# Hybrid conv/pool decoder block: the conv output's transposes moved from TensorE to the DMA crossbar

## The chip, the cores and the metric

The kernel runs on all 8 cores of one Trainium2 chip. Each core computes 2048 of the 16384 token rows (four sequences of 4096, half a sequence per core) and needs nothing from the other cores; a core that has the second half of a sequence also gets the 32 rows before it. The metric is the device time in microseconds (us) of the slowest core.

## What is computed

The reference, cut to the branch that matters here (`C_CONV` = 1024 channels):

```python
def conformer_conv_branch(u_glu, dw_kernel, dw_bias, ln_g, ln_b, w_out):
    a, gate = jnp.split(u_glu, 2, axis=-1)
    u = a * jax.nn.sigmoid(gate)
    u = depthwise_causal_conv(u, dw_kernel, dw_bias)   # width 31
    u = layer_norm(u, ln_g, ln_b)                      # per token, over channels
    u = jax.nn.swish(u)
    return u @ w_out
...
merged = g_conv * y_conv + g_pool * y_pool
h = h + rms_norm(merged @ w_o, mix_post_g)
```

`y_pool` comes from a pooling branch of the same projection, `g_conv` and `g_pool` are sigmoid gates, and a squared-ReLU MLP of width 4096 follows.

## The kernel before, in words

All of it is one program per core. A small recorder (class `KB`) keeps one list of instructions for each engine in the order in which the Python code emits them, works out from the memory cells which semaphore waits each needs, and emits the lists. So an engine (and each DMA queue: SP's for `LOAD` and `DTR`, POOL's for `WLOAD`) does its work strictly in program order, and an instruction that waits holds up all behind it on the same engine. TensorE's matmuls are recorded at line 220 (`MM`) and its transposes, which are matmuls against an identity, at line 223 (`TR`); ScalarE's activations at line 238; the crossbar transposes, issued from SP, at line 263 (`DTR`).

The stages in order: RMS norm and transposes of x; pooling projection; GLU projection (`glu_pair`), whose result goes through `DTR` (`conv_in`, lines 567 to 572: for each of 8 channel slabs one transpose of a 16-partition halo and one of a 128 x 2048 tile); the depthwise conv as matmuls (`cv_mm`); then the stage of this change, lines 724 to 747; then the conv branch's projection, the output projection and the MLP.

The conv leaves its output in `cv`, indexed [partition m, slab cc, r, channel c], where the token is 16 m + r. There tokens lie on the partitions, which suits the layer norm: `ln_stat`, `ln_fin` and `ln_norm` run on VectorE from a list of background steps (`bgd`), of which `pump(n)` does the next n; there are 16 `ln_norm` steps, one for each r, over all slabs. The projection after it (`wco`) needs channels on the partitions: that is `s_t`, which lies in the same memory as `cv`, slab for slab.

The stage itself is the first pass of `gated` (line 684), 4 token blocks by 8 output slabs, 32 calls, here numbered 0 to 31 (number 8 blk + cc). Each call has two times 8 matmuls of 128 x 512 on `weff` and `wgp`, into a pair of the 8 PSUM banks; then a tanh on ScalarE (line 691) and one VectorE operation that multiplies (line 694), after which the pair is free again. Call n+4 uses the pair of call n.

In blocks 2 and 3, after every odd cc (calls 17, 19, ..., 31), `cv_t3` (line 711) handles one slab: 16 TensorE transposes of 128 x 128 into two PSUM banks, then two ScalarE activations that compute silu with the layer norm's gain and bias and write the slab of `s_t` in place. The last slab follows call 31, and right behind it the second pass begins (line 840): `gated` on `wco` and `s_t`, whose first 8 matmuls read slabs 0 to 7 in turn.

Behind the first pass SP's queue has `LOAD(gb1)`, `LOAD(gb2)` (lines 750, 751) and three loads of x (line 755). `gb1` lies at the start of the scratch region `TP`.

Of the kernel before, what the change touches and what calls it, by code (L numbers as in the profile page):

```python
# [8 lines left out]
BF16 = mybir.dt.bfloat16  # L9
AF = mybir.ActivationFunctionType  # L10
# [16 lines left out]
TP = RM + 8 * NT  # L27
# [143 lines left out]
def build_program():  # L171
# [20 lines left out]
    with ExitStack() as es:  # L192
# [3 lines left out]
        identb = T("identb", [128, 128], BF16)  # L196
# [7 lines left out]
        ps = es.enter_context(nc.psum_tensor("ps", [128, 8, 512], F32))  # L204
        kb = KB()

        def av(off, *dims, dt=BF16):
            n = int(np.prod(dims))
            v = arena[:, off:off + (n if dt is BF16 else 2 * n)]
            if dt is not BF16:  # L210
                v = v.bitcast(dt)
            if len(dims) > 1:
                names = ["d%d" % i for i in range(len(dims))]
                v = v.rearrange("p (" + " ".join(names) + ") -> p " + " ".join(names),
                                **{a: d for a, d in zip(names[:-1], dims)})
            return v
# [5 lines left out]
        def TR(o, i, idn):  # L222
            kb.op("pe", lambda e: e.transpose(o, i, idn), [i, idn], [o])  # L223

        def ACT(o, i, func, bias=None, scale=None, accum=None):
            kw = {}
            rd, wr = [i], [o]
            if bias is not None:
                kw["bias"] = bias
                rd.append(bias)  # L230
            if scale is not None:
                kw["scale"] = scale
                if not isinstance(scale, float):
                    rd.append(scale)
            if accum is not None:
                kw["accum_out"] = accum
                wr.append(accum)
            kb.op("act", lambda e: e.activation(out=o, in_=i, func=func, **kw), rd, wr)  # L238
# [22 lines left out]
        def DTR(o, i):  # L261

            return kb.op("sp", lambda e: e.dma_start_transpose(out=o, in_=i), [i], [o], dma=True)

        def WLOAD(o, src, after=()):
            return kb.op("pool", lambda e: e.dma_start(out=o, in_=src), [], [o], dma=True, after=after)  # L266
# [3 lines left out]
        def banks(n):  # L270
            b = -(-st["bank"] // n) * n % 8
            st["bank"] = (b + n) % 8
            return b
# [9 lines left out]
        cv = av(RS, 8, 16, 128)  # L283
        s_t = av(RS, 8, NT)
# [3 lines left out]
        def slot(i, *dims):  # L288
            return av(RW + i * SLOT, *dims)
# [15 lines left out]
        kc = [av(RW + 4608 + b * 768, 48, 16) for b in range(2)]  # L305
        hg = [av(TP + b * 2048, 2048)[0:16, :] for b in range(2)]
        Wc = slot(6, 16, 3, 128)
        bias_bc = av(RW + 7 * SLOT + 2048, 1024, dt=F32)
        pwT = av(RW + SLOT + 2048, 4, 2, 256)
        pwf = av(RM + 4096, 4, 2, 256, dt=F32)  # L310
# [75 lines left out]
        def vcol(base, cc):  # L386
            return vec[:, base + cc:base + cc + 1]
# [51 lines left out]
        def pump(n):  # L439
            for _ in range(n):  # L440
                if bgd:
                    bgd.popleft()()
# [163 lines left out]
        def ln_stat(half, r):  # L606
            i = cv[:, 4 * half:4 * half + 4, r, :]
            o = bnst[:, r, half, :]
            kb.op("dve", lambda e: e.bn_stats(o, i), [i], [o])  # L609
# [5 lines left out]
        def conv_steps(pair):  # L615

            def spread(cc, cs):
                for c in cs:
                    cv_w(cc, c)

            def fin(cc):
                if cc + 2 < 8:
                    conv_load(cc + 2)
                cv_mm(cc)

            out = []
            for cc in (2 * pair, 2 * pair + 1):
                out += [lambda cc=cc: spread(cc, (0, 1, 2)), lambda cc=cc: spread(cc, (3, 4, 5)),
                        lambda cc=cc: spread(cc, (6, 7)), lambda cc=cc: fin(cc)]
            return out  # L630
# [53 lines left out]
        def gated(cc, blk, wy, src, wgate, first):  # L684
            b = banks(2)
            for k in range(8):
                MM(ps[:, b, :], wy[:, k, cc * 128:(cc + 1) * 128], src[:, k, blk * 512:(blk + 1) * 512], k == 0, k == 7)
            for k in range(8):
                MM(ps[:, b + 1, :], wgate[:, k, cc * 128:(cc + 1) * 128], uT[:, k, H + blk * 512:H + (blk + 1) * 512], k == 0, k == 7)
            sg = sigslot()  # L690
            ACT(sg, ps[:, b + 1, :], AF.Tanh, scale=0.5)
            m = m1(blk, cc)
            if first:
                STT(m, sg, 1.0, ps[:, b, :], ALU.add, ALU.mult)
            else:
                STT(sg, sg, 1.0, ps[:, b, :], ALU.add, ALU.mult)
                TTE("dve", m, sg, m, ALU.add)
# [9 lines left out]
        def ln_norm(r):  # L707
            v = cv[:, :, r, :]
            TS(v, v, bnag[:, r, 0:1], ALU.subtract, lnr[:, r:r + 1], ALU.mult)

        def cv_t3(cc):
            sv = s_t[:, cc, :].rearrange("p (m r) -> p m r", r=16)
            pbs = []
            for half in range(2):
                b = banks(1)
                pb = ps[:, b, :].bitcast(BF16)
                pbs.append(pb)
                for r8 in range(8):
                    TR(pb[:, r8 * 128:(r8 + 1) * 128], cv[:, cc, half * 8 + r8, :], identb[:])
            for half in range(2):  # L720
                ACT(sv[:, :, half * 8:half * 8 + 8], pbs[half].rearrange("p (r m) -> p m r", r=8), AF.Silu,
                    bias=vcol(8, cc), scale=vcol(0, cc))

        for blk in range(4):
            steps = deque(conv_steps(3) if blk == 0 else [])
            for cc in range(8):
                gated(cc, blk, weff, z, wgp, True)
                if blk == 0:
                    pump(2)
                    if cc == 0:  # L730
                        steps.popleft()()
                        steps.popleft()()
                    if steps:
                        steps.popleft()()
                    if cc == 6:
                        for r in range(16):
                            bgd.append(lambda r=r: ln_stat(1, r))
                        bgd.append(ln_fin)
                        for r in range(16):
                            bgd.append(lambda r=r: ln_norm(r))  # L740
                elif blk == 1:
                    pump(5)
                elif cc % 2 == 1:
                    cv_t3((blk - 2) * 4 + cc // 2)
            if blk == 0:
                WLOAD(wgc, w_in_v[:, :, 3072:4096])
                WLOAD(wo, wo_v)
# [247 lines left out]
```

How the kernel before makes its waits and increments, by code:

```python
            def body(h, items=items):  # L156
                for waits, fn, ev, dma in items:
                    for sk, v in waits.items():
                        h.wait_ge(sems[sk], rank[sk][v] if sk in rank else v)
                    if fn is None:
                        continue
                    inst = fn(h)
                    if dma:
                        inst.then_inc(sems[ev[0]], 16)
                    elif ev[1] in rank[ev[0]]:
                        inst.then_inc(sems[ev[0]], 1)
```

## Time and profile before

| | us |
|---|---|
| runs of the kernel, median of three | 975.74 |
| the profiled execution's own time | 976.0 |
| its span, first to last instruction, slowest core | 974.4 |
| spans of the 8 cores | 971.7 to 974.4 |
| TensorE busy within the span | 949.2 |

The profile shows one execution. The span is some 1.6 us shorter than that execution's own time, and this execution lies 0.3 us above the median of the three runs. A busy TensorE means that matmuls were in its pipeline; one matmul's listed duration overlaps the next one's, so the cost of a group on the path is read from the starts of the groups, or from the chain of waits, and not from the mean duration. TensorE's granted clock was 1.00 in the stage of the change, the higher of its two levels (2.4 GHz).

### The profile page before, as it was taken

What the parts mean: (1) busy time and instruction counts of PE and PEld (TensorE: products, weight loads), DVE (VectorE), ACT (ScalarE), POOL (GpSimd) and SP (SyncE); (2) the same over time, 40 slices, a digit from 0 to 9 for tenths busy, and PEclk for the clock granted to TensorE, in tenths of its full rate; (3) what the DMA queues carried; (4) which work ended last, traced back from release to release, by engine and by line L of the source; (5) the groups of instructions that cost most, each with busy time, mean ns of one, the idle gap of its engine ahead of it and who ended that gap; (6) DMA issues with size and microseconds to landing.
All of it is one profiled execution on the core that took longest, in us unless ns stands there. A gap on an engine that the chain in (4) does not pass through costs nothing.

```text
span 974.4 us, 14114 instructions; the slowest of 8 cores (971.7 to 974.4 us)
## 1 busy us (share of the span) xinstructions
PE 949.2 (97%) x4971; PEld 484.2 (50%) x4971; DVE 451.3 (46%) x767; ACT 277.6 (28%) x531; POOL 62.6 (6%) x112
## 2 busy tenths in 40 slices
PE   7789999999999999999999999999999999999996
PEld 4655666665545544444444444444444444444444
DVE  4478886575482114566666630344223431244222
ACT  4553111132114431333335530233202330133211
POOL 1010001000010000121213200000000000000000
PEclk9999999999999999999999999999999999999999
DMA  9995165976780021759989995220022001210021
GB/s 183 253 146 74 17 89 105 143 109 115 118 140 1 1 87 15 143 117 191 168 190 178 196 197 90 87 87 1 1 87 87 1 1 44 87 43 1 1 86 66
DMA packets 93111, 91.21 MB, mean 94 GB/s; under 512 B 43601, under 2 KB 74577, under 8 KB 92914
## 3 DMA queue, kind: packets, MB, share of 16 engines
q0 software_dynamic: 32416, 35.13, 26.2%
q1 hardware_dynamic: 60626, 55.18, 21.1%
q8 instruction: 41, 0.67, 0.3%
q14 instruction: 28, 0.23, 0.1%
HBM read 98.88 MB, written 16.84 MB: 119 GB/s over the span
## 4 chain that ended last, share of the span: by engine, by line
PE 91%; DMA 3%; DVE 3%; ACT 1%; issue 1%; DVEq 0%; ACTq 0%; SPq 0%
PE ps L220 90%; DMA arena<-w_in 2%; DMA arena<-xh 1%; ACT arena L238 1%; PE ps L223 1%; DVE arena L246 1%; DVE arena L250 1%; DVE arena L477 0%; DMA arena<-arena 0%; DVE arena L241 0%; ACT sm L238 0%; DVE arena L256 0%; DVEq L159 0%; DVE sm L400 0%; ACTq L159 0%
## 5 line engine op out<-in xcount | busy, mean ns | idle before, releaser
L220 PE MATMUL ps<-arena 128*128 128x512 bf16 (+4 forms) x4731 | 937.9, 360 | 13.9 <-DVE arena L246 2.8
L220 PEld LDWEIGHTS ps<-arena 128*128 128x128 bf16 (+1 forms) x4731 | 470.1, 103 | 473.4 <-issue 25.7
L238 ACT ACTIVATE arena<-ps 128x512 bf16<-128x512 f32 (+5 forms) x346 | 203.0, 593 | 622.1 <-PE ps L220 467.0
L246 DVE TENSOR_SCALAR ps<-ps 128x512 f32<-128x512 f32 x128 | 89.1, 699 | 110.9 <-PE ps L220 110.2
L241 DVE TENSOR_TENSOR ps<-ps,arena 128x512 f32<-128x512 f32 (+1 forms) x65 | 43.6, 688 | 176.1 <-ACT arena L238 175.6
L250 DVE SCALAR_TENSOR_TENSOR arena<-arena,ps 128x512 bf16<-128x512 f32 (+1 forms) x64 | 43.9, 686 | 133.0 <-ACT arena L238 111.0
L241 DVE TENSOR_TENSOR arena<-ps,arena 128x512 bf16<-128x512 f32 (+2 forms) x52 | 42.3, 830 | 35.6 <-ACT arena L238 29.6
L238 ACT ACTIVATE arena<-arena 128x1024 bf16<-128x1024 f32 (+1 forms) x33 | 34.8, 1054 | 46.3 <-DVE arena L250 35.8
L250 DVE SCALAR_TENSOR_TENSOR arena<-ps,sm,arena 128x512 f32<-128x512 f32 (+1 forms) x65 | 45.1, 737 | 5.0 <-DVE sm L400 3.0
L250 DVE SCALAR_TENSOR_TENSOR arena<-arena,sm 128x1024 bf16<-128x1024 f32 (+1 forms) x33 | 42.3, 1282 | 4.3 <-POOL sm L396 2.4
L241 DVE TENSOR_TENSOR arena<-arena 128x512 bf16<-128x512 f32 (+2 forms) x56 | 38.4, 690 | 4.3
L246 DVE TENSOR_SCALAR arena<-arena,vec 128x768 bf16<-128x768 bf16 (+1 forms) x72 | 27.7, 413 | 2.7
L266 POOL DMA_DIRECT2D arena<-w_in x14 | 12.6, 909 | 156.7 <-DMA arena<-arena 137.3
L223 PE MATMUL ps<-identb,arena 128*128 128x128 bf16 (+1 forms) x240 | 16.9, 220 | 3.7 <-DVE arena L250 2.1
L266 POOL DMA_DIRECT2D arena<-w_ff x16 | 13.5, 852 | 106.7 <-PE ps L220 99.4
L238 ACT ACTIVATE arena<-ps,vec 128x1024 bf16<-128x1024 bf16 x16 | 19.3, 1204 | 2.5 <-PE ps L223 1.7
L609 DVE BATCH_NORM_STATS2 bnst<-arena 128x6 f32<-128x512 bf16 x32 | 19.9, 679 | 0.0
L223 PEld LDWEIGHTS ps<-identb,arena 128*128 128x128 bf16 (+1 forms) x240 | 14.9, 99 | 9.0 <-issue 5.8
L400 DVE RECIPROCAL sm<-sm 128x1 f32<-128x1 f32 (+1 forms) x33 | 5.3, 162 | 29.2 <-ACT sm L238 17.4
L396 POOL TENSOR_TENSOR sm<-sm,mhalf 128x1 f32<-128x1 f32 x32 | 18.2, 567 | 5.0 <-POOL sm L395 0.4
L250 DVE SCALAR_TENSOR_TENSOR arena<-arena 128x512 bf16<-128x512 f32 x24 | 16.5, 687 | 1.2
L477 DVE TENSOR_TENSOR_SCAN arena<-arena,scr 128x512 f32<-128x512 f32 x12 | 15.3, 1278 | 3.6 <-ACT arena L238 3.6
(34 smaller groups left out, 91.3 us busy)
## 6 DMA issues: line engine op xcount, KB each, us to landing
arena<-xh SPq DMA_DIRECT2D x32, 512.0 KB, 8.6
arena<-w_ff POOLq DMA_DIRECT2D x16, 1024.0 KB, 27.8
out<-arena SPq DMA_DIRECT2D x31, 512.0 KB, 3.1
arena<-out SPq DMA_DIRECT2D x16, 512.0 KB, 4.1
arena<-w_in POOLq DMA_DIRECT2D x12, 512.0 KB, 13.1
arena<-w_in POOLq DMA_DIRECT2D x2, 2048.0 KB, 17.2
arena<-gb SPq DMA_DIRECT2D x4, 512.0 KB, 6.4
arena<-w_pool_out POOLq DMA_DIRECT2D x2, 1024.0 KB, 23.1
```

The lines of the kernel that those rows point to most:

```text
L220: kb.op("pe", lambda e: e.matmul(o, lhsT=l, rhs=r, start=start, stop=stop), [l, r], [o])
L223: kb.op("pe", lambda e: e.transpose(o, i, idn), [i, idn], [o])
L238: kb.op("act", lambda e: e.activation(out=o, in_=i, func=func, **kw), rd, wr)
L241: kb.op(eng, lambda e: e.tensor_tensor(out=o, in0=a, in1=b, op=op), [a, b], [o])
L246: kb.op("dve", lambda e: e.tensor_scalar(out=o, in0=a, scalar1=s1, scalar2=s2, op0=op0, **kw), rd, [o])
L250: kb.op("dve", lambda e: e.scalar_tensor_tensor(out=o, in0=a, scalar=s, in1=b, op0=op0, op1=op1), rd, [o])
L266: return kb.op("pool", lambda e: e.dma_start(out=o, in_=src), [], [o], dma=True, after=after)
L396: kb.op("pool", lambda e: e.tensor_tensor(out=o, in0=o, in1=mhalf[:, 0:n], op=ALU.pow), [o, mhalf[:, 0:n]], [o])
L400: kb.op("dve", lambda e: e.reciprocal(o, o), [o], [o])
L477: kb.op("dve", lambda e: e.tensor_tensor_scan(so, pc[:, lo:lo + n], pc[:, lo - w:lo - w + n], init, ALU.add, ALU.subtract), rd, [so])
L609: kb.op("dve", lambda e: e.bn_stats(o, i), [i], [o])
```

## The change

`cv_t3` issues one crossbar transpose (`DTR`) of a whole 128 x 2048 slab, from SP, into one of two new buffers `s_r`, and a new function `silu` computes the activation from that buffer in one ScalarE instruction of 2048 elements per partition. The buffers lie at the start of `TP` (the first one where `gb1` is loaded later). The first two slabs are sent off after call 15, the last of block 1, behind a `pump(32)` that does any normalization step still left. From call 18 to call 25, each call is followed by the silu of one slab (0 to 7) and the transpose of the slab two further on, which goes into the buffer that this silu has read.

```diff
+        s_r = [av(TP + b * 2048, 16, 128) for b in range(2)]
...
         def cv_t3(cc):
-            sv = s_t[:, cc, :].rearrange("p (m r) -> p m r", r=16)
-            pbs = []
-            for half in range(2):
-                b = banks(1)
-                pb = ps[:, b, :].bitcast(BF16)
-                pbs.append(pb)
-                for r8 in range(8):
-                    TR(pb[:, r8 * 128:(r8 + 1) * 128], cv[:, cc, half * 8 + r8, :], identb[:])
-            for half in range(2):
-                ACT(sv[:, :, half * 8:half * 8 + 8], pbs[half].rearrange("p (r m) -> p m r", r=8), AF.Silu,
-                    bias=vcol(8, cc), scale=vcol(0, cc))
+
+            DTR(s_r[cc % 2], cv[:, cc, :, :].rearrange("p r c -> p (r c)"))
+
+        def silu(cc):
+            ACT(s_t[:, cc, :].rearrange("p (m r) -> p m r", r=16), s_r[cc % 2].rearrange("p r m -> p m r"), AF.Silu, bias=vcol(8, cc), scale=vcol(0, cc))
...
                 elif blk == 1:
                     pump(5)
-                elif cc % 2 == 1:
-                    cv_t3((blk - 2) * 4 + cc // 2)
+                    if cc == 7:
+                        pump(32)
+                        cv_t3(0)
+                        cv_t3(1)
+                elif 8 * blk + cc in range(18, 26):
+                    n = 8 * blk + cc - 18
+                    silu(n)
+                    if n + 2 < 8:
+                        cv_t3(n + 2)
```

## Rows read from the trace of the kernel before

**Rows 1.** The page's part 1: busy time, share of the span, instructions.

```profile
PE 949.2 (97%) x4971; PEld 484.2 (50%) x4971; DVE 451.3 (46%) x767; ACT 277.6 (28%) x531; POOL 62.6 (6%) x112
```

**Rows 2.** TensorE's waits, 358 to 970 us: total us, times, longest.

```profile
PE ps L220 <- ACT arena L238: 1.2, 1, 1.2
```

**Rows 3.** Chain of waits, 290 to 370 us: start, us on the chain, what.

```profile
299.86 0.89 PE ps L223 x16
300.75 6.91 PE ps L220 x32
...
354.46 0.91 PE ps L223 x16
...
355.45 1.21 ACT arena L238
...
356.75 1.21 ACT arena L238
```

**Rows 4.** Timeline of TensorE, 352 to 372 us: start, us, what, idle before.

```profile
355.19 1.67 PE L220 MATMUL ps<-arena 128*128 128x512 bf16 x7
358.10 14.19 PE L220 MATMUL ps<-arena 128*128 128x512 bf16 x65 [1.24 <-ACT arena L238]
```

**Rows 5.** Timeline of VectorE, 255 to 355 us.

```profile
293.43 0.55 DVE L246 TENSOR_SCALAR arena<-arena,bnag,lnr 128x1024 bf16<-128x1024 bf16 x1
300.84 0.69 DVE L250 SCALAR_TENSOR_TENSOR arena<-arena,ps 128x512 bf16<-128x512 f32 x1 [2.77 <-PE ps L223]
```

**Rows 6.** Line 263, crossbar transposes, fastest and slowest of eight 128 x 2048 ones.

```profile
L263 SPq DMA_TRANSPOSE arena<-arena x1: 2056/2056/2056, 158.5 to 158.5; - x1
DMA to landing us min/median/max: 4.3/4.3/4.3
...
L263 SPq DMA_TRANSPOSE arena<-arena x1: 1992/1992/1992, 124.3 to 124.3; - x1
DMA to landing us min/median/max: 5.8/5.8/5.8
```

**Rows 7.** Stretches: busy us of each engine, clock, DMA share, GB/s.

```profile
194.00:202.00 8.00, 8.00 (x39) 5.05 (x38) 5.20 (x11) 3.13 (x4) 0.00 (x0) 1.00 0.42 78
292.00:316.00 24.00, 24.00 (x146) 12.22 (x145) 6.06 (x11) 9.96 (x12) 0.00 (x0) 1.00 0.00 1
316.00:340.00 24.00, 24.00 (x153) 12.45 (x151) 4.35 (x7) 11.17 (x14) 0.00 (x0) 1.00 0.00 1
```

**Rows 8.** DMA issues, 259 to 292 us, KB, us to landing; timeline of POOL.

```profile
260.40 0.88 POOL L266 DMA_DIRECT2D arena<-w_o  x1 [0.25 <-issue]
...
arena<-w_o POOLq DMA_DIRECT2D x1, 2048.0 KB, 29.2
```

**Rows 9.** Groups by line and shape, 292 to 358 us: busy us, mean ns.

```profile
L238 ACT ACTIVATE arena<-ps,vec 128x1024 bf16<-128x1024 bf16 x16 | 19.3, 1204 | 2.5 <-PE ps L223 1.7
```

**Rows 10.** The page's part 5: activations that read SBUF.

```profile
L238 ACT ACTIVATE arena<-arena 128x1024 bf16<-128x1024 f32 (+1 forms) x33 | 34.8, 1054 | 46.3 <-DVE arena L250 35.8
```

**Rows 11.** Timeline of ScalarE, 299 to 306 us.

```profile
300.07 0.60 ACT L238 ACTIVATE arena<-ps 128x512 f32<-128x512 f32 x1 [2.86 <-PE ps L220]
300.83 1.28 ACT L238 ACT_TABLE_LOAD   x1 [0.17 <-PE ps L223]
```

**Rows 12.** Timeline of SP's queue, 120 to 130 and 180 to 355 us.

```profile
119.03 7.22 SPq L263 DMA_TRANSPOSE arena<-arena  x3
...
236.89 116.27 SPq L259 DMA_DIRECT2D arena<-gb  x2
353.20 2.27 SPq L259 DMA_DIRECT2D arena<-xh  x3
```

**Rows 13.** Line 263, the slowest 128 x 1024 transpose, and queues, 480 to 490 us.

```profile
L263 SPq DMA_TRANSPOSE arena<-arena x1: 3954/3954/3954, 483.8 to 483.8; - x1
DMA to landing us min/median/max: 12.6/12.6/12.6
...
q0 software_dynamic: 1157, 1.17, 92.0%
```

## The prediction

> **What bounds the kernel now.** I read the busy times first: TensorE is busy 97% of the span, VectorE 46%, ScalarE 28% [rows 1]. So the end is set by how much work TensorE has and by the few places where it waits, and the reader should look at nothing else until TensorE has been accounted for. Second, TensorE's waits: behind 358 us it waits once, for 1.2 us [rows 2]. Whatever moves 358 us earlier moves the end earlier by as much, unless a new wait appears. Third, the chain of waits through the stage of the change. It alternates strictly between two groups: 32 matmuls (two `gated` calls) for 6.91 us, and the 16 transposes of a slab for 0.89 us [rows 3]. There are eight such transpose groups, the last of 0.91 us. So the transposes are not hidden, they stand on the chain between matmuls. Last, TensorE's own timeline at the end of the stage: after the last transposes it does 7 matmuls of the second pass, slabs 0 to 6, and stands still for 1.24 us until ScalarE has finished the two silus of slab 7, 1.21 us each on the chain [rows 3, 4].
>
> **What the change takes away.** The 128 transposes: 7 x 0.89 + 0.91 = 7.14 us of chain [rows 3]. Their listed durations would give another figure, because matmuls overlap; the chain has the price. Then the stall before the second pass, 1.24 us [rows 4]: it exists because slab 7 is transposed behind the last call, and the new order has its silu six calls earlier. Together 8.38 us. Nothing else is late at that point: `wco` was loaded before this stage, `wgc` and `wo` too (29.2 us after an issue at 260.4 us, so by 290 us [rows 8]).
>
> The two PSUM banks that each slab took are no longer allocated; eight slabs took 16, two full turns of eight, so every later call gets the banks it had.
>
> **What it adds, and why I cost it at nothing.** Four parts.
>
> *The start.* `pump(32)` has nothing to do: the list's last normalization runs at 293.43 us for 0.55 us, in the slot of call 14 [rows 5]. So SP may issue slab 0 at 294.0. Call 17 ends at 299.70 us and its tanh starts at 300.07 [rows 11]; a call takes 6.91 / 2 = 3.45 us [rows 3]. Call 18's tanh, with no transposes ahead, is due at 303.52.
>
> *The transposes.* The same kernel already sends eight 128 x 2048 tiles through the crossbar (`conv_in`). They take 4.7, 5.8, 4.7, 4.3, 4.7, 5.5, 4.7 and 4.4 us from issue to landing, mean 4.85, fastest and slowest in [rows 6]; the issue itself holds SP some 2 us. I take 4.9. These ran beside other traffic: the engines were 42% busy while a few of them passed, and in the new place they are 0% busy [rows 7], so contention should be lower. Bounds for the landing: the fastest of the eight below, 4.3 us, and above the slowest crossbar transpose of the trace, 12.6 us, for a tile of half the size while weight loads kept the engines 92% busy [rows 13].
>
> A rule that speaks against this step: the Trainium skill, page "VectorE: DVE Perf Modes", section "The three transpose paths", lists 390 ns for a 128 x 128 bf16 transpose on TensorE and 1309 ns through the DMA crossbar, and its rules for authors send such a transpose to TensorE wherever a PSUM destination will do. By that price a slab of 16 blocks would take 16 x 1.309 = 20.9 us if they pass one after another, an estimate from that page. The trace disagrees with both figures: 0.89 / 16 = 0.056 us for a block on TensorE [rows 3] and at most 5.8 us for a slab [rows 6].
>
> *ScalarE.* Sixteen silus of 1.204 us go [rows 9], eight of 2048 elements come. Below: a 1024-element activation from SBUF takes 1.054 us and a 512-element tanh 0.60 [rows 10, 11], so 0.45 us per 512 elements and 1.054 + 2 x 0.45 = 1.95 us. Above: the trace shows no activation that reads SBUF in 256-byte steps; were each element to cost double, 2 x 1.95 = 3.9. Two of the present silus, which read PSUM in the same pattern, make 2.41, and I take 2.4 as the nearest row. With a tanh of 0.60 that is 3.0 of the 3.45 us of a call: ScalarE fits, narrowly. The table load of 1.28 us before the first silu stays [rows 11].
>
> *The loop.* The new wait is a ring: a silu waits for its slab, and the transpose two further on waits for that silu. One turn is 4.9 + 2.4 = 7.3 us, while two calls take 6.9. So the silus drift by 0.4 us per turn. Behind a waiting silu stands the next call's tanh, behind that the VectorE operation, behind that the PSUM pair, which TensorE needs four calls later. Step by step: tanh 18 ends at 304.12, table load to 305.40, silu 0 to 307.8; slab 2 lands at 312.7 (silu due 311.0), slab 4 at 320.0, slab 6 at 327.3, silu 6 ends at 329.7. The tanh of call 25 behind it was due at 327.67: 2.0 us late, the worst of all. In general, with landing time L, this tanh is 0.83 + 3 x (L - 4.5) us late. What can it afford? A pair is normally free when the VectorE operation ends, 300.84 + 0.69 = 301.53 for call 17, 1.83 us after its last matmul [rows 5], and is needed three calls later, 10.35 us. Slack 8.5 us, against 2.0 used. So TensorE does not see the ring at all until L passes 7.1 us. Slab 7's silu ends at about 332.7, and the second pass now starts near 348.0 (299.70 + 14 x 3.45): 15 us to spare.
>
> *SP's queue.* Behind the six waiting transposes stand `gb1`, `gb2` and three loads of x. `gb1` now waits for silu 6, near 330 us; `gb2` waited for the matmuls of the stage's end anyway and held the x loads until 353.2 us [rows 12]. They follow TensorE as before. POOL's queue has no load in this stage. If that cover were gone, the first output tile would wait for them, but it comes a whole block later.
>
> **The sum.** Against the profiled execution: 976.0 - 7.14 - 1.24 = 967.6 us. That execution lies 0.3 us above the median of the three runs, so by the median it would be 967.4; I keep 967.6. The gain is 0.9%, below the 2% that a measurement of this kernel can tell from no change.
>
> **Rivals.**
>
> *A. The ring is too slow (slower side).* Landing takes 12.6 us, as for the transpose beside the weight loads [rows 13]. Then tanh 25 is 0.83 + 3 x 8.1 = 25.1 us late, 16.6 beyond the slack, and the time is 967.6 + 16.6 = 984.2. It decides from L = 7.1 us on, and the gain is all gone at 16.9 us of lateness, L = 9.9. Against it: the DMA engines idle in this stage [rows 7], and no 128 x 2048 tile took over 5.8 us. Chance 0.05.
>
> *B. Slabs pass one at a time.* If the crossbar did not overlap or start them sooner, at 12.6 us each the eighth lands at 294.0 + 8 x 12.6 = 394.8, its silu ends at 397.2, call 26's pair is free 1.5 us later, at 398.7, and call 30, due at 341.1, waits 57.6 us: 1025. Against it: the rows named under A, and from 119.0 us on SP issued three transposes in 7.2 us [rows 12], the last of them the slowest of the eight [rows 6]; one after another at 12.6 us does not fit that. Chance 0.02. By the estimate of 20.9 us from the Trainium skill's page above this would be 8 x 8.3 = 66 us worse still; the trace's 5.8 us speaks against it.
>
> *C. Part is given back.* Silus of 3.9 us, or landings near 8 us: a ring turn of 4.9 + 3.9 = 8.8 us drifts 1.9 per turn, and ScalarE at 3.9 + 0.6 = 4.5 us per call falls 1.05 us per call behind, 8 us over the stage. With the table load that is about 9 to 10 us late, 1 to 2 beyond the slack; L = 8 gives 11.3 late, 2.8 beyond. Time 968.5 to 970.5. For it: ScalarE fits only narrowly. Chance 0.08.
>
> *D. The end does not move.* Something later, now 8.4 us sooner, waits for a transfer that starts at its old time: 976. Against it: behind 358 us TensorE has no such wait [rows 2], and the loads follow it. Chance 0.03.
>
> **How the numbers follow.** The forecast, 967.6, has 0.82. Its own spread is small: the chain terms are read to 0.02 us each, runs differ by about 0.5 us. The range takes in C and some unseen cost: 966.3 to 971.5; outside lie A, B and D (0.10) and the tails. Faster by over 2% (below 956.2) would need more than the stage holds: 0.01. Slower by over 2% (above 995.3) is B and a bad part of A: 0.03. Within 2%: 0.96.
>
> **What would show it.** Right: no transposes between the matmul groups from 299 us on; two calls every 6.91 us through calls 16 to 31; no wait of TensorE before the second pass, which starts near 348; eight transposes on line 263 between 294 and 326 us landing in 4.3 to 5.8 us; eight silus near 2.4 us; some tanhs up to 2 us late; TensorE's total busy time some 7 us lower. Wrong: landings over 7 us, silus over 3 us, or TensorE waiting for VectorE or ScalarE between 310 and 345 us.

## The result, and the profile after

The changed kernel takes 967.84 us (median of four runs), the kernel before 975.67 (median of four). The ratio is 0.9918 with a 95% interval of 0.9898 to 0.9937: some 7.8 to 8.0 us less, clear of zero, and below the 2% at which a verdict of faster is given. One of the four executions of before took 1109.9 us in a slow state that some executions of any kernel fall into, with a lower granted clock on some cores; the ratio leaves it out. The profiled execution took 967.8 us; its slowest core, core 0, has a span of 966.3 us. The forecast was 967.6.

A total that fits does not show that its terms fit. One of them was badly off here, and the profile shows which. First the page's part 1 of the changed kernel:

```profile
PE 937.5 (97%) x4758; PEld 477.7 (49%) x4843; DVE 451.8 (47%) x767; ACT 287.9 (30%) x523; POOL 62.5 (6%) x112
```

Against [rows 1], TensorE lost 11.7 us of busy time, but this must not be read as a gain. 4731 weight loads of line 220 are listed and only 4646 of its matmuls: 85 matmul records are missing in this trace. ScalarE is the surprise: eight activations fewer, and 10.3 us more busy time. The groups by line and shape from 292 to 350 us, core 0, say why (busy us, mean ns of one; then the idle time before them and what ended it):

```profile
L220 PE MATMUL ps<-arena 128*128 128x512 bf16 x258 | 57.0, 379 | 1.4 <-DVE arena L250 1.2
L238 ACT ACTIVATE arena<-arena,vec 128x2048 bf16<-128x2048 bf16 x8 | 31.3, 3918 | 1.7 <-DMA arena<-arena 1.7
```

A silu of 2048 elements takes 3.92 us, not the 2.4 that I took, where two of the old ones took 2.41 [rows 9]. And TensorE waits for 1.2 us, for VectorE's line 250, which the forecast said it would not. Its timeline on core 0:

```profile
284.64 51.53 PE L220 MATMUL ps<-arena 128*128 128x512 bf16 x233
336.67 3.61 PE L220 MATMUL ps<-arena 128*128 128x512 bf16 x16 [0.50 <-DVE arena L250]
340.96 34.26 PE L220 MATMUL ps<-arena 128*128 128x512 bf16 x155 [0.67 <-DVE arena L250]
```

The transposes between the matmuls and the stall of 1.24 us before the second pass [rows 3, 4] are gone, and two shorter waits have come at another place. The same view on core 1 has no wait at all:

```profile
284.74 90.60 PE L220 MATMUL ps<-arena 128*128 128x512 bf16 x419
```

So the cores differ. A measure that all have: the time from the tanh of call 17 (the last before the first silu in either kernel) to the tanh of call 32, the first of the second pass, read from each core's ScalarE timeline. I call it the stage. Without any wait it is 15 calls of 3.453 us, 51.80 us. It varies far less than whole runs do: the time at which the stage begins differs by up to 2.8 us between the cores of one of these two executions. Each figure below is read from one profiled execution.

| | stage, 8 cores (us) | median | TensorE waits in it (us) |
|---|---|---|---|
| before | 60.28 to 60.29 | 60.29 | 1.2 on each core |
| after | 53.30, 51.80, 52.42, 51.89, 51.80, 51.83, 52.41, 52.51 | 52.15 | 1.2, 0, 0.5, 0, 0, 0, 0.4, 0.6 |

The stage became 8.14 us shorter at the median, 6.99 to 8.49 by core. Line 263 (the crossbar transposes) in the stage, core 0 and then core 1; the line that begins with ACT says who waited for them, us and times:

```profile
L263 SPq DMA_TRANSPOSE arena<-arena x8: 1693/1962/3721, 292.4 to 331.0; - x8
...
  ACT arena L238: 1.7, 1
...
DMA to landing us min/median/max: 4.2/4.4/6.0
```

```profile
L263 SPq DMA_TRANSPOSE arena<-arena x8: 1746/1990/2852, 292.0 to 329.1; - x8
...
DMA to landing us min/median/max: 4.3/4.4/4.8
```

The landings are close to what the eight of before promised [rows 6]; over all cores those took 4.2 to 6.2 us. On core 0 one of them, slab 2, took 6.0 us; ScalarE waited 1.7 us for it, on core 1 not at all. And ScalarE's timeline on core 1, where TensorE never waits:

```profile
298.06 0.60 ACT L238 ACTIVATE arena<-ps 128x512 f32<-128x512 f32 x1 [2.86 <-PE ps L220]
301.51 0.60 ACT L238 ACTIVATE arena<-ps 128x512 f32<-128x512 f32 x1 [2.86 <-PE ps L220]
302.13 1.28 ACT L238 ACT_TABLE_LOAD   x1
303.43 3.90 ACT L238 ACTIVATE arena<-arena,vec 128x2048 bf16<-128x2048 bf16 x1
...
333.66 3.90 ACT L238 ACTIVATE arena<-arena,vec 128x2048 bf16<-128x2048 bf16 x1
337.47 1.05 ACT L238 ACTIVATE arena<-ps 128x512 f32<-128x512 f32 x2
```

The tanh of call 26 was due at 298.06 + 9 x 3.453 = 329.14 and ran at 337.47, 8.3 us late. Calls 18 to 25 cost ScalarE about 4.3 us each, 0.85 more than TensorE's 3.45; with the table load of 1.28 us before the first silu, eight such calls make 8 x 0.85 + 1.28 = 8.1 us. The slack that the prediction had worked out was 8.5 us. This core came through with 0.2 us to spare; on core 0 the same tanh was 9.9 us late, and TensorE waited.

My reading was then: the two savings are as forecast; silus read in 256-byte steps are slow and nearly fill the slack; whether a core waits is left to the landing of slab 2. The experiments test each part.

### The profile page after: what moved, and what is told of

Read it like the earlier page. It is cut to its first block, busy times and chain, and to the rows that moved or that the text cites. A ratio compares the mean times of both kernels' runs of the same rounds, so it can differ in the third digit from the quotient of the medians.

```text
span 966.3 us, 13780 instructions; the slowest of 8 cores (962.9 to 966.3 us)
## 1 busy us (share of the span) xinstructions
PE 937.5 (97%) x4758; PEld 477.7 (49%) x4843; DVE 451.8 (47%) x767; ACT 287.9 (30%) x523; POOL 62.5 (6%) x112
## 4 chain that ended last, share of the span: by engine, by line
PE 90%; DMA 3%; DVE 2%; ACT 2%; issue 2%; DVEq 0%; ACTq 0%; SPq 0%
PE ps L220 90%; ACT arena L238 2%; DMA arena<-w_in 2%; DMA arena<-xh 1%; DVE arena L241 1%; DVE arena L246 1%; DVE arena L250 0%; PE ps L223 0%; DVE arena L478 0%; ACT sm L238 0%; ACTq L159 0%; DVEq L159 0%; DVE ps L241 0%; DVE arena L256 0%; DVEq L192 0%
## 5 line engine op out<-in xcount | busy, mean ns | idle before, releaser
L238 ACT ACTIVATE arena<-arena,vec 128x2048 bf16<-128x2048 bf16 x8 | 31.3, 3918 | 1.7 <-DMA arena<-arena 1.7
L396 POOL TENSOR_SCALAR sm<-sm 128x1 f32<-128x1 f32 x32 | 7.1, 221 | 133.0 <-DVE sm L241 67.6
L238 ACT ACTIVATE sm<-sm,epst 128x1 f32<-128x1 f32 (+1 forms) x33 | 9.7, 295 | 16.1 <-DVE sm L241 14.5
```

Source lines behind the costliest of these rows:

```text
L396: kb.op("pool", lambda e: e.tensor_scalar(out=o, in0=i, scalar1=EPS[epsc], scalar2=None, op0=ALU.add), [i], [o])
```

## The experiments

There are eight. What tells them apart is the stage, by core, which repeats to 0.01 us where nothing waits.

### The changed kernel again

> No edit: the changed kernel once more, on the same chip as the experiments. Theory (lateness of 8.2 to 8.3 us from the silus, slack 8.5, and a landing of over 4.8 us for slab 2 takes the rest): stage 51.80 us on the cores where that slab lands within 4.8 us and up to 1.5 more where it does not, and which cores these are differs from the first profile or not by the landing alone; whole kernel 966 to 968.5. Rival: the waits belong to fixed cores whatever the landing.

Measured: 967.50 us; stage 51.80 to 52.88, median 51.92. TensorE's waits are not on the same cores: on 3, 5 and 7 now, where the first profile had 0, 2, 6 and 7. The third transpose of each core (slab 2, the one that follows silu 0), from both profiles:

| landing of slab 2 (us) | stage (us) |
|---|---|
| 4.2 to 4.6 (8 cores) | 51.80 to 51.89 |
| 4.7 | 51.98 |
| 5.1, 5.1, 5.2, 5.2 | 52.42, 52.41, 52.51, 52.51 |
| 5.3 | 52.59 |
| 5.6 | 52.88 |
| 6.0 | 53.30 |

Above 4.5 us, and not only above the 4.8 expected, each microsecond of landing is a microsecond of the stage. So it is the landing and not the core that decides (rival out). The landing itself was predicted within bounds; why it scatters between 4.2 and 6.0 us stays open. In these two profiles SP's issue is long too where the landing is (3.7 us on core 0, 1.8 on core 1), but in the contiguous version below that slab landed in 6.0 to 6.1 us on three cores after issues of 1.7 to 1.9 us.

### Four buffers instead of two

```diff
-s_r = [av(TP + b * 2048, 16, 128) for b in range(2)]
+s_r = [av(o, 16, 128) for o in (TP, TP + 2048, RM + 12288, RM + 14336)]
...
-DTR(s_r[cc % 2], ...)
+DTR(s_r[cc % 4], ...)
...
+cv_t3(2)
+cv_t3(3)
...
-if n + 2 < 8:
-    cv_t3(n + 2)
+if n + 4 < 8:
+    cv_t3(n + 4)
```

> Edit: four buffers instead of two, so the transposes run four slabs ahead and the ring is open. Theory R+ring (ScalarE's silus use up 8.3 of the 8.5 us of slack and a slab that lands late adds the rest): no silu waits for a landing, silus stay at 3.92 us, worst tanh about 8.3 us late, no TensorE waits or at most 0.2 us, stage 51.8 us on all cores; whole kernel 966.5 to 967.5. Rival A of the prediction (the ring itself sets the pace): silus still wait for landings, or the lateness falls far below 8 us. Rival S (ScalarE's rate alone is over the slack): waits of TensorE stay near 1.2 us.

Measured: 967.78 us; stage 51.80 on all eight cores, no wait of TensorE on any. Who waited for whom, 298 to 345 us, core 0:

```profile
ACT arena L238 <- PE ps L220: 8.6, 3, 2.9
ACT arena L238 <- DVE arena L250: 0.5, 1, 0.5
```

No line names the DMA any more, though some landings still took 6.0 us. The silus stayed at 3.9 us, and the latest tanh was 8.1 us late on every core. So the ring was not the pace (rival A of the prediction is out); ScalarE's rate is, and it stops just short of the slack (so rival S is out too). The whole kernel lies a little above the 966.5 to 967.5 expected and within 0.1% of the change. That is no contradiction: what the median core had to win was 0.35 us, less than the scatter of the cores' starts.

### Contiguous silu, in two versions

First, the read made contiguous and the write stepped:

```diff
-ACT(s_t[:, cc, :].rearrange("p (m r) -> p m r", r=16), s_r[cc % 2].rearrange("p r m -> p m r"), AF.Silu, ...)
+ACT(s_t[:, cc, :].rearrange("p (m r) -> p r m", r=16), s_r[cc % 2], AF.Silu, ...)
```

> Edit: the silu walks its input in the order in which it lies (contiguous read of the buffer) and writes the slab in 32-byte steps instead. Theory R (the 256-byte-step read is what makes a silu take 3.92 us): the silu falls to 2.0 to 2.4 us, the worst tanh is about 2 us late instead of 8.3 to 9.9, no core waits, tanh of call 17 to tanh of call 32 is 51.8 us on all eight cores (52.15 median, up to 53.30 with the change as made); whole kernel 966 to 967.5. Rival L (2048 elements out of SBUF cost that much in any order, or a strided write costs as much): the silu stays near 3.9 us and four of eight cores keep waits of 0.4 to 1.2 us; 967.8.

Measured: 1009.65 us, ratio 1.0347 (1.0330 to 1.0364); stage 91.7 to 94.7. A clear miss: neither theory had it. Groups from 290 to 400 us, then a piece of TensorE's timeline, both on core 3, the slowest:

```profile
L238 ACT ACTIVATE arena<-arena,vec 128x2048 bf16<-128x2048 bf16 x8 | 71.9, 8993 | 0.0
```

```profile
325.88 6.53 PE L220 MATMUL ps<-arena 128*128 128x512 bf16 x16 [4.67 <-DVE arena L250]
335.19 5.30 PE L220 MATMUL ps<-arena 128*128 128x512 bf16 x16 [2.77 <-DVE arena L250]
```

A silu that writes in 32-byte steps takes 9.0 us. ScalarE then needs 9.3 us per call with a silu, the slack is gone after two of them, and TensorE waits in each later call, 26.8 us in all; 16 matmuls take 5.0 to 6.5 us in place of 3.45 between the waits, at a granted clock of 0.66 to 0.83 averaged over stretches of 10 us (1.00 is its higher level, 0.50 its lower). The slower matmuls do not set the pace: the stretches begin 9.3 us apart (325.88, 335.19) whatever their matmuls take, and that is ScalarE's time per call. This is the price of a lateness that does not fit, paid in full. Since the theory predicted 2.0 to 2.4 us, it had to be asked whether steps are the cause at all. So, both sides contiguous:

```diff
-ACT(s_t[:, cc, :].rearrange("p (m r) -> p m r", r=16), s_r[cc % 2].rearrange("p r m -> p m r"), AF.Silu, ...)
+ACT(s_t[:, cc, :].rearrange("p (r m) -> p r m", r=16), s_r[cc % 2], AF.Silu, ...)
```

> Edit: the silu reads its buffer in the order in which it lies and writes the slab in the same order; this leaves out putting the tokens back in order (the slab stays r-major). Theory R (with the read in 256-byte steps a silu took 3.92 us and with the write in 32-byte steps 9.0 us: steps on either side are what costs): 2048 contiguous elements take 1.95 to 2.1 us, ScalarE needs 2.6 of the 3.45 us of a call, the worst tanh is under 2 us late, no TensorE wait, stage 51.8 us on all cores. Rival L (2048 elements SBUF to SBUF take 3.9 us by their number): silu 3.9 us, tanhs 8 us late.

Measured: 967.10 us, stage 51.80 on all cores. Groups from 296 to 345 us:

```profile
L238 ACT ACTIVATE arena<-arena,vec 128x2048 bf16<-128x2048 bf16 x8 | 16.7, 2091 | 3.4 <-DMA arena<-arena 3.4
```

2.09 us: the 2048 elements from SBUF to SBUF are not dear by number, the steps are. (This version leaves out putting the tokens back in order, so it measures what the steps cost and can't replace the change.) The latest tanh of any core is 2.2 us late, a little over the 2 expected, and silus now do wait for their slabs, 3.4 us in all on this core and up to 6.5 on others. That is the kind of wait the prediction had described for silus of 2.4 us, and it is harmless. But it does not build up: a turn of the ring, 4.4 + 2.1 = 6.5 us, is shorter than two calls, and the waits of silus 2, 4 and 6 on core 4 shrink, 1.35, 1.12 and 0.91 us.

### The silus spread out

```diff
-elif 8 * blk + cc in range(18, 26):
-    n = 8 * blk + cc - 18
+elif 8 * blk + cc in (17, 19, 20, 22, 24, 25, 27, 29):
+    n = (17, 19, 20, 22, 24, 25, 27, 29).index(8 * blk + cc)
```

> Edit: the change with its two buffers, but the silus after calls 17, 19, 20, 22, 24, 25, 27 and 29 instead of 18 to 25. Theory (ScalarE's 4.29 us per call with a silu against TensorE's 3.45 makes the lateness, 0.84 us per call in a row): with 13 calls to carry 8 silus the lateness stays under 4 us, no silu sets a wait of TensorE, stage 51.8 us on all eight cores; whole kernel as with four buffers, 967 to 968. Rival A (landings of the ring set the pace): waits on some cores as before.

Measured: 967.41 us; stage 51.80 on all eight cores. The latest tanh is 2.3 us late on every core, within the 4 us expected. Two buffers and the slow silu are enough if ScalarE has calls without a silu in between. From ScalarE's timeline on core 0, silu 6 and what follows:

```profile
334.33 3.91 ACT L238 ACTIVATE arena<-arena,vec 128x2048 bf16<-128x2048 bf16 x1
338.14 0.59 ACT L238 ACTIVATE arena<-ps 128x512 f32<-128x512 f32 x1
340.74 0.60 ACT L238 ACTIVATE arena<-ps 128x512 f32<-128x512 f32 x1 [2.02 <-PE ps L220]
```

ScalarE waits for TensorE again before the next tanh: it has caught up.

### The order alone, and the crossbar alone

The change has two parts, the way of the transposes and the place of the silus. The kernel before with TensorE's transposes at the new places:

```diff
-elif cc % 2 == 1:
-    cv_t3((blk - 2) * 4 + cc // 2)
+elif 8 * blk + cc in range(18, 26):
+    cv_t3(8 * blk + cc - 18)
```

> Edit: the kernel before with its TensorE transposes and its silus out of PSUM, but one slab after each of calls 18 to 25, as in the change. Theory: only the stall before the second pass goes: stage 60.29 - 1.24 = 59.05 us, whole kernel 974.0 to 975.0; ScalarE has 2.5 + 0.6 us of work in the 4.35 us that a call with a slab takes, so it keeps up. Rival (the order has a price of its own: the transposes' PSUM banks leave the calls only three pairs): new waits of TensorE, stage 59.5 us or more.

Measured: 974.30 us, ratio 0.9983 (0.9973 to 0.9993); stage 58.94 to 58.95 on all cores, no wait of TensorE, so the rival is out. Its timeline on core 3, the slowest:

```profile
303.09 1.06 PE L223 MATMUL ps<-identb,arena 128*128 128x128 bf16 x16
303.98 3.62 PE L220 MATMUL ps<-arena 128*128 128x512 bf16 x16
307.43 1.06 PE L223 MATMUL ps<-identb,arena 128*128 128x128 bf16 x16
...
334.41 37.93 PE L220 MATMUL ps<-arena 128*128 128x512 bf16 x175
```

One call and one transpose group take 307.43 - 303.09 = 4.34 us, 3.45 + 0.89, eight times; then matmuls without a gap into the second pass. The order by itself is worth 60.29 - 58.95 = 1.34 us, and the transposes 58.95 - 51.80 = 7.15.

The crossbar with the silus at the old places:

```diff
-elif 8 * blk + cc in range(18, 26):
-    n = 8 * blk + cc - 18
+elif 8 * blk + cc in (17, 19, 21, 23, 25, 27, 29, 31):
+    n = (17, 19, 21, 23, 25, 27, 29, 31).index(8 * blk + cc)
```

> Edit: the crossbar transposes as in the change, but the silus at the old places, after calls 17, 19, ..., 31. Theory: the transposes' 7.14 us still go, the stall before the second pass comes back and grows, because one silu of 3.92 us takes the place of two that ended 2.73 us after the last transposes: tanh end plus 3.92 puts slab 7 about 5.0 us behind call 31, the 7 matmuls cover 1.5, stall 3.5 us; stage about 55.4 us, whole kernel 971 to 972. Rival (the stall is not tied to the place of the last silu): stage 51.8 to 53 us.

Measured: 972.74 us, ratio 0.9966 (0.9956 to 0.9977); stage 55.13 to 57.02. Before the second pass TensorE waits, on core 2:

```profile
352.25 20.04 PE L220 MATMUL ps<-arena 128*128 128x512 bf16 x77 [3.17 <-ACT arena L238]
```

The wait is 3.2 us on all cores, close to the 3.5 expected. But the whole kernel came out above the 971 to 972 expected, and only three cores have a stage of 55.13; on the other five it is 1.3 to 1.9 us longer. Stretches of 4 us (busy times of PE, PEld, DVE, ACT and POOL, then the granted clock, DMA share, GB/s) on core 0, whose wait ends at 350.13 us, and on core 2, where it ends at 352.25:

```profile
348.00:352.00 4.00, 1.87 (x9) 0.97 (x10) 0.00 (x0) 1.98 (x1) 0.00 (x0) 1.00 1.02 344
352.00:356.00 4.00, 4.00 (x21) 1.81 (x19) 1.38 (x2) 0.71 (x2) 0.00 (x0) 1.00 0.10 40
```

```profile
352.00:356.00 4.00, 3.75 (x9) 1.39 (x10) 0.00 (x0) 0.11 (x1) 0.00 (x0) 0.50 0.98 359
356.00:360.00 4.00, 4.00 (x15) 1.61 (x14) 1.38 (x2) 0.60 (x1) 0.00 (x0) 0.75 0.13 51
```

After the same wait of 3.2 us, core 0 went on at 2.4 GHz and core 2 at the lower level, 1.2 GHz. The loads that pass at that time do not tell the two apart: the DMA engines are as busy around the end of the wait on core 0 (share 1.02) as on core 2 (0.98). The clock accounts for the loss: on core 1 it was 0.50 from the end of the wait at 352.08 us to 355.02 us, half of these 2.9 us is 1.5, and its stage is 1.44 us longer than 55.13. So a wait of this length can cost about half as much again, on some cores and not on others; which cores it hits stays open.

### One buffer

```diff
-s_r = [av(TP + b * 2048, 16, 128) for b in range(2)]
+s_r = [av(TP, 16, 128)]
...
-                        cv_t3(1)
...
-if n + 2 < 8:
-    cv_t3(n + 2)
+if n + 1 < 8:
+    cv_t3(n + 1)
```

> Edit: one buffer instead of two, so each transpose waits for the silu before it and each silu for its transpose. Theory (a ring of landing plus silu, hidden until the slack of 8.5 us is used): one turn is 4.5 + 3.92 + 0.1 = 8.5 us per slab against 3.45 per call, silu 7 ends some 68 us after the tanh of call 17, call 30 waits for it, TensorE waits about 28 us in total and more if its clock falls; stage 80 to 84 us, whole kernel 995 to 1000. Rival B (slabs pass faster when alone, or the silus catch up): stage under 70 us.

Measured: 998.87 us, ratio 1.0235 (1.0218 to 1.0253); stage 80.72 to 84.20, median 81.62. Waits from 298 to 377 us, core 0:

```profile
ACT arena L238 <- DMA arena<-arena: 29.7, 7, 5.9
PE ps L220 <- DVE arena L250: 22.5, 6, 6.6
```

Three pieces of TensorE's timeline on core 0:

```profile
335.13 4.95 PE L220 MATMUL ps<-arena 128*128 128x512 bf16 x16 [2.96 <-DVE arena L250]
343.40 5.30 PE L220 MATMUL ps<-arena 128*128 128x512 bf16 x15 [3.32 <-DVE arena L250]
351.65 5.22 PE L220 MATMUL ps<-arena 128*128 128x512 bf16 x16 [2.95 <-DVE arena L250]
```

This is the prediction's ring with a turn longer than TensorE's call: seven waits for a landing on ScalarE, and from the third slab on TensorE waits too. The stage is 29.8 us longer at the median than without waits. Of that 21.1 to 22.5 us are listed waits, less than the 28 expected; in the rest TensorE ran matmuls more slowly. That is not a second cause in the ring: the stretches begin 8.3 us apart, which is its turn (4.2 us for the landing, 3.9 for the silu and some 0.2 between), and matmuls that take longer only take the place of waiting, as in the version with the stepped write.

## Why the prediction was right, point by point

**The transposes, 7.14 us: right.** Shown by the version with the order alone against the stage without waits: 7.15 us. The chain of waits had the price. The Trainium skill's 390 ns for a 128 x 128 transpose on TensorE (page "VectorE: DVE Perf Modes", section "The three transpose paths") would have made the saving seven times too large, an estimate from that page, and its 1309 ns per block on the crossbar, one after another, a kernel far slower than before. No run bears out either as a price in a stream: 0.056 us on the chain, and in the changed kernel slabs of 16 blocks landing in 4.2 to 6.0 us.

**The stall, 1.24 us: right.** The order alone gave 1.34, so with the transposes 8.49 against 8.38 forecast. That run has no wait before the second pass; the run with the silus at the old places has one again, of 3.2 us.

**The ring: right in its form, wrong in what set the pace.** In the first profile silu 2 waited for its slab on four of eight cores, 0.8 to 1.7 us, and no later silu did; ScalarE was always late enough by then that the slabs had landed. The lateness grew at ScalarE's rate, until call 26 and not 25, to 8.1 us without any landing wait. The formula with the landing time is not shown by any run: only the contiguous version has the waits that it is made of, and there a turn is shorter than two calls and the latest tanh was call 21, 22 or 24, not 25. Its end, the slack of 8.5 us, is shown below.

**ScalarE, 2.4 us a silu: wrong.** This is the step that failed: "the nearest row" was two old silus, and the upper bound of 3.9 was what came, 3.92. The old ones read PSUM in the same steps, and that row did not carry over to SBUF. A row of the same access pattern is no nearer than a row of the same memory when neither has both. The runs show 2.09 us contiguous, 3.92 with the read in 256-byte steps, 9.0 with the write in 32-byte steps. The Trainium skill, page "Advanced Engine Details and Errata", section "Memory Cachelines", says that SBUF accesses which each go to another 16-byte line lose speed. The runs agree with it. I had not weighed that rule.

**The slack of 8.5 us: right, and it is why the total fitted.** Over both profiles, cores whose latest tanh was at most 8.5 us late have stages of 51.80 to 51.89; at 8.6 us it is 51.98, and from 9.0 us on they wait. My error on ScalarE made lateness 8.3 us in place of 2.0, and the slack took nearly all of it. That it did was luck, not forecast. So "TensorE does not see the ring" was true on four cores, by 0.4 us or less. The mechanism on every core is that of rival C, silus of 3.9 us, to which I had given a chance of 0.08; on the other four cores part was given back as it says (0.6 to 1.5 us). It came out milder than C's 9 to 10 us late because a call costs ScalarE 4.3 us and not 3.9 + 0.6 = 4.5: in the timeline on core 1 most operations start some 0.1 us before the one ahead of them ends. By the prediction's own signs of being wrong, two of three came: silus over 3 us, and TensorE waiting for VectorE between 310 and 345 us.

The total of 967.84 is the sum of two right savings and a small, scattered loss. That it lies within 0.3 us of the forecast is in part chance too: in the profiled executions the slowest core before (core 7) began the stage at 300.07 us and the slowest after (core 0) at 298.39. These 1.7 us lie ahead of the stage, in work that the change does not touch, and they hide the 1.5 us that core 0 gave back.

**SP's queue and what comes later: right.** Behind the stage the changed kernel has no wait of TensorE on any core, and from the tanh of call 32 to the end it takes 614.0 to 614.6 us, the kernel before 614.0 to 615.0: the end moved with the stage (rival D is out). Rivals A and B are out: the second slab is issued before the first has landed, and slabs land in 4.2 to 6.0 us.

The versions with four buffers or spread silus remove the loss in the stage on every core. In time of the whole kernel, 967.41 to 967.78, they can't be told from the change (967.50 and 967.84).

## What to carry to other kernels

Work that moves off the path can come back through the engine that takes it over: sum that engine's work per turn of the loop, not per stage, add what comes once (a table load here), and compare the lateness that it builds up with the slack that the buffers give. Where the sum ends within a few tenths of the slack, expect cores to differ, and spread the work or add buffers before measuring. A reordering belongs on the side where the steps are cheapest (here the read), and an activation's price should be taken from a row with the same memory and the same step on each side, or kept as a range.

## What had not been expected of the hardware

An activation of 2048 bf16 elements per partition, SBUF to SBUF, took 2.09 us contiguous, 3.92 us with 256-byte steps in the read and 9.0 us with 32-byte steps in the write. The order of the loops in one instruction made a factor of 2.3 between the last two, and 42 us of kernel time.

After a wait of 3.2 us in the same place of the same program, three cores kept a granted clock of 1.00 and five did not; on core 2 it was 0.50 over the next 4 us.
